# Two tiles' relative-position bands loaded as one overlapping stretch in the second attention layer

## What is computed

```
rel = Q_BLOCK + i - m
bias = rel_bias[relative_bucket(rel * dilation)]      # one number for each head and distance
s = einsum(q, k) * scale + bias
s = where(valid, s, NEG_INF)
lse = logsumexp(s);  p = exp(s - lse);  o = einsum(p, v)
o = sum over groups of softmax(lse over groups) * o
```

## Time and profile before

| what | us |
|---|---|
| median of 3 launches (lowest, highest) | 759.71 (758.87, 760.59) |
| the profiled execution's own time | 757.09 |
| its span | 755.3 |
| PE busy in the span | 744.8 (99%) |
| DVE, ACT, POOL busy | 531.9, 416.7, 175.4 |
| TensorE's mean granted clock | 0.998 of full speed |

### The profile page before, as it was taken

The page is one execution under the profiler, slowest core; times in us unless marked ns, Lnnn a source line. Parts: engine busy times, 40 slices in busy tenths (PEclk is TensorE's granted clock), DMA queues, the critical chain, the costliest instruction groups (busy, mean ns, idle before and its releaser), DMA issues.

```text
span 755.3 us, 13376 instructions
## 1 busy us (share of the span) xinstructions
PE 744.8 (99%) x4616; PEld 639.5 (85%) x4616; DVE 531.9 (70%) x766; ACT 416.7 (55%) x619; POOL 175.4 (23%) x298
## 2 busy tenths in 40 slices
PE   9999999999999999999999999999999999999996
PEld 7999987888888888999898898898878888888884
DVE  5888997776766657777777677677557675666653
ACT  4766667444343344865855867766576434433421
POOL 1000001225100000146664664666502000000000
PEclk9999999999999999999999999999999999999999
DMA  8645585699976675559798897897743797767602
GB/s 251 198 126 162 181 245 186 187 275 231 239 250 202 184 223 136 164 157 242 182 219 175 207 190 194 190 223 210 242 140 98 252 277 217 213 192 233 228 14 56
DMA packets 190756, 147.16 MB, mean 195 GB/s; under 512 B 38521, under 2 KB 179425, under 8 KB 190721
## 3 DMA queue, kind: packets, MB, share of 16 engines
q1 hardware_dynamic: 153344, 131.45, 57.0%
q10 hardware_dynamic: 30592, 7.84, 6.4%
q0 software_dynamic: 6784, 7.41, 6.1%
HBM read 138.02 MB, written 1.11 MB: 184 GB/s over the span
## 4 chain that ended last, share of the span: by engine, by line
PE 61%; issue 16%; POOL 10%; DMA 7%; DVE 3%; ACT 1%; POOLq 1%; SPq 0%; DVEq 0%; ACTq 0%
PE ps L1283 16%; PE ps L1284 15%; PE ps L1285 15%; DMA ones<-bias_rows 4%; POOL work L480 4%; POOL work L499 2%; PE ps L1289 2%; PE ps L1291 2%; PE ps L1290 2%; POOL ones L482 2%; DMA work<-work 2%; POOL work L497 2%; DVE w_lo L852 1%; PE ps L1360 1%; PE ps L1377 1%
## 5 line engine op out<-in xcount | busy, mean ns | idle before, releaser
L852 DVE TENSOR_TENSOR w_lo<-raw,w_hi 128x2048 fp32r<-128x2048 f32 (+2 forms) x144 | 279.8, 1961 | 70.7 <-ACT w_hi L542 70.7
L542 ACT ACTIVATE w_hi<-raw 128x2048 fp32r<-128x2048 f32 (+2 forms) x144 | 233.2, 1639 | 99.4 <-DMA raw<-in_w_kv_b 38.0
L1283 PE MATMUL ps<-w_hi,xt 128*128 128x512 f32 x352 | 137.6, 391 | 0.0
L1285 PE MATMUL ps<-w_hi,xt 128*128 128x512 f32 x352 | 137.0, 389 | 0.0
L1284 PE MATMUL ps<-w_lo,xt 128*128 128x512 f32 x352 | 137.0, 389 | 0.0
L716 ACT ACTIVATE work<-ps,stat 128x256 f32<-128x256 f32 x44 | 21.0, 477 | 155.4 <-PE ps L1285 151.2
L449 POOL TENSOR_SCALAR stat<-stat 128x1 f32<-128x1 f32 x15 | 9.6, 639 | 405.8 <-ACT work L558 381.7
L1283 PE MATMUL ps<-w_hi,ot 128*128 128x512 f32 x240 | 95.0, 396 | 0.1
L1284 PE MATMUL ps<-w_lo,ot 128*128 128x512 f32 x240 | 93.6, 390 | 0.0
L1285 PE MATMUL ps<-w_hi,ot 128*128 128x512 f32 x240 | 93.5, 390 | 0.0
L480 POOL DMA_DIRECT2D work<-bias_rows x128 | 74.9, 587 | 43.5 <-DVE ot L1135 26.7
(11 more groups left out here) (157 smaller groups left out, 1274.2 us busy)
## 6 DMA issues: line engine op xcount, KB each, us to landing
raw<-in_w_gate_up SPq DMA_DIRECT2D x88, 512.0 KB, 5.0
raw<-in_w_kv_b SPq DMA_DIRECT2D x96, 256.0 KB, 4.5
raw<-in_w_down SPq DMA_DIRECT2D x22, 1024.0 KB, 5.2
raw<-in_w_q_b SPq DMA_DIRECT2D x48, 256.0 KB, 4.6
raw<-in_w_qkv_a SPq DMA_DIRECT2D x23, 512.0 KB, 5.2
raw<-in_w_o_a SPq DMA_DIRECT2D x4, 1024.0 KB, 6.9
work<-bias_rows POOLq DMA_DIRECT2D x128, 32.0 KB, 3.6
raw<-in_w_o_b SPq DMA_DIRECT2D x4, 1024.0 KB, 5.2
```

What stands on the lines that cost most here:

```text
L542: act.activation(w_hi[:, s % CUT, 0:size(s)], raw[:, s % RAW, 0:size(s)], ACT.Copy).then_inc(hi_made, 1)
L852: dve.tensor_tensor(w_lo[:, c, 0:n], raw[:, s % RAW, 0:n], w_hi[:, c, 0:n].bitcast(F32), ALU.subtract).then_inc(lo_made, 1)
L1283: mm(out, xs[0], ws[0], start=start, stop=False)
L1285: return mm(out, xs[1], ws[0], start=False, stop=stop)
```

## The change

The two tiles' bands become one stretch of `SPAN` = 64 + 32 = 96 words for each run: `band` is now [128, 4 runs, 96], and tile t reads words 32t to 32t + 63 of each run. The diagonal stretch becomes 96 words in the same way and has room of its own in `work`, for all heads. A head has four transfers of 32 partitions of 4 runs of 96 words (48 KB) and four of 32 partitions of one run of 96 words (12 KB). The additions have the same shapes. The wait for `rows_done` ahead of the loop is gone, since `ones` is no longer overwritten. `work` is 32 words a partition smaller.

```
-WORK = 6912
+WORK = 6880
+SPAN = RUN + HR * (NT - 1)
...
-                         [[(2 * R - 1) * 2 * RUN, NH], [1, HR], [HR, NT], [2 * RUN, R], [1, RUN]]) for r in range(R)]
+                         [[(2 * R - 1) * 2 * RUN, NH], [1, HR], [2 * RUN, R], [1, SPAN]]) for r in range(R)]
...
-        band = carve(NT * SEQ).rearrange("p (t s) -> p t s", t=NT)
-        early_band, own_band = (v.rearrange("p (t n) -> p t n", t=NT) for v in (halves_in[:, 0:NT * RUN], ones[:, :]))
+        band = carve(R * SPAN).rearrange("p (c s) -> p c s", c=R)
+        own_band = carve(SPAN)
...
-                    for t in range(NT):
-                        pool.dma_start(band[at_, t].rearrange("p (c n) -> p c n", c=R),
-                                       bands[r][ds(h, 1)][:, :, t].rearrange("h m c n -> (h m) c n")).then_inc(band_in, 16)
-                    pool.dma_start(own_[at_], own_bands[ds(h, 1)].rearrange("h m t n -> (h m) t n")
-                                   ).then_inc(band_in, 16)
-                pool.wait_ge(band_in, (h * 16 + 16) * (R * (NT + 1)))
+                    pool.dma_start(band[at_], bands[r][ds(h, 1)].rearrange("h m c n -> (h m) c n")).then_inc(band_in, 16)
+                    pool.dma_start(own_band[at_], own_bands[ds(h, 1)].rearrange("h m n -> (h m) n")).then_inc(band_in, 16)
+                pool.wait_ge(band_in, (h * 16 + 16) * (2 * R))
...
-                    distances = band[:, t, ::-1].rearrange("p (c u n) -> p u c n", c=R, u=NT)
+                    reach = slice(HR * t, HR * t + RUN)
+                    distances = band[:, ::-1, reach][:, :, ::-1].rearrange("p c (u n) -> p u c n", u=NT)
...
-            pool.wait_ge(rows_done, 2)
```

More of the change, by code:

```diff
@@ L130, in build @@
         bands = [bass.AP(bias_rows.tensor, bias_rows.offset + 2 * RUN * r,
-                         [[(2 * R - 1) * 2 * RUN, NH], [1, HR], [HR, NT], [2 * RUN, R], [1, RUN]]) for r in range(R)]
+                         [[(2 * R - 1) * 2 * RUN, NH], [1, HR], [2 * RUN, R], [1, SPAN]]) for r in range(R)]
         own_bands = bass.AP(bias_rows.tensor, bias_rows.offset + 2 * RUN * (R - 1),
-                            [[(2 * R - 1) * 2 * RUN, NH], [1, HR], [HR, NT], [1, RUN]])
+                            [[(2 * R - 1) * 2 * RUN, NH], [1, HR], [1, SPAN]])
         raw = sb("raw", [P, RAW, UNIT])
@@ L495, in head_bias @@
                     to, blocked = part(bias[b], t), part(mask_b, t)
-                    distances = band[:, t, ::-1].rearrange("p (c u n) -> p u c n", c=R, u=NT)
+                    reach = slice(HR * t, HR * t + RUN)
+                    distances = band[:, ::-1, reach][:, :, ::-1].rearrange("p c (u n) -> p u c n", u=NT)
                     pool.tensor_tensor(to[0], blocked[0], distances[:, 0:t + 1], ALU.add)
-                    distances = own_[:, t:t + 1, ::-1].rearrange("p o (u n) -> p u o n", u=NT)
+                    distances = own_band[:, reach][:, ::-1].rearrange("p (o u n) -> p u o n", o=1, u=NT)
                     inst = pool.tensor_tensor(to[1], blocked[1], distances[:, 0:t + 1].broadcast_to(
```

1 line of the change is left out of this document (removed).

## The result

| | kernel before | changed kernel |
|---|---|---|
| median of 22 launches each (lowest, highest) | 758.65 (754.59, 761.97) | 760.84 (759.45, 762.96) |
| the profiled execution's own time | 757.09 | 760.09 |
| its span | 755.3 | 758.3 |

The ratio is 1.0034, with a 95% interval of 1.0019 to 1.0048: the change makes the kernel slower by 0.34%, about 2.6 us (the two medians lie 2.2 us apart). The forecast was a gain of 2.4 us. The launches of the kernel before spread over 7.4 us and those of the changed kernel over 3.5; of the kernel before there is one profile, so what its other launches looked like inside is not known. A second set on another chip gave 1.0044 (1.0026 to 1.0062).

The account below looks back on a forecast made before the run. PE was taken to bound the kernel, busy 744.8 of 755.3 us. Gains of 1.59 us (pair 6, last transposes) and 0.8 (pairs 1 to 3) made 2.4: 759.71 - 2.4 = 757.3 us, range 755.9 to 759.7.

Parts of the forecast that it names:

- What bounds the kernel: Layer two's attention: PE is full, 28.70 us is its own length of a pair, POOL can return only what PE loses.
- Four issues less a head: POOL's transfers: 2.3 us less issuing, landing kept at 5.01 us, so a head takes 12.2 us instead of 14.54.
- The lead, and the DVE waits go to nothing: Attention: bias ready 10 to 13 us before DVE's `peaks` wants it; DVE's three waits, 14.6 us in all, vanish.
- What this returns: Attention on PE: 0.99 us of pair 6, 0.60 at the last transposes, and 0.8 of pairs 1 to 3's 1.02.
- the loss isn't there in ordinary launches: Rival: the pause in head 10 was an accident of the profiled execution; about 759.3 us, chance 0.18.
- Nothing behind it takes it back: Behind the attention: PE's list is fixed, DVE and ACT were idle there, so the 1.59 us stays gained.
- The slower rival: The pause stands before POOL's 133rd transfer, now the third `load_post`, with no lead: +4.0 us, 763.7, chance 0.06.
- The additions: POOL's additions read runs 96 words apart instead of 64; even 1 us more on each of four fits the lead.
- the collision: Each pair: POOL's additions behind `peaks` meet DVE's `w_lo`, 0.5 us of DVE; counted as nothing, bound 3.5 us.

Follow-up runs that it names:

- the kernels of 9.99 us: The changed kernel with one of head 1's transfers split, or with 8, 40, 116 or 750 more transfers on POOL: 759.31, 759.69, 758.71, 759.13, 1098.75 us.

## Why the prediction was wrong, step by step

**What bounds the kernel**: right. PE's own length of a pair, 28.70 us, is what all pairs but two now show, and those read 28.75 and 28.78.

**Four issues less a head**: right in direction, short in size. A head took 4.70 + 2.93 us for issues and landing against 4.7 + 5.01 expected. The 5.01 was kept from heads of twelve transfers; in the loop with eight the landings that POOL waited for took 1.7 to 3.8 us. Heads 0 and 1, outside the loop and also with eight, took 5.40 and 4.24, and with five larger transfers a head it was up to 6.1, so what shortens them is not shown.

**The lead, and the DVE waits go to nothing**: right. DVE waits for POOL nowhere, POOL waits 60.8 us for DVE's peaks.

**What this returns**: 1.59 + 0.8 = 2.4 expected, 2.72 measured from pair 0 to the outputs. The size was right, and of the cause only a part. I laid the loss on 0.4 us a pair of a POOL that is too slow, with the pause on top. But with twelve transfers a head and pauses of 1.79 us in head 6 and 5.93 in head 12 the attention takes the same 218.3 us, pairs 1 to 3 included; with 3.49 in head 3 and 6.81 in head 12 it takes 222.3. So it is the place of a pause, and its length, that decide, against a lead that eight transfers make large and twelve leave small. That the pace of twelve transfers a head costs 0.4 us a pair by itself is a second step that didn't hold: a kernel with that pace and its pauses elsewhere doesn't lose it. What exactly lengthened pairs 1 to 3 in the kernel before, I can't say. The rival "the loss isn't there in ordinary launches" had half of this: it said that without the pause POOL would be late nowhere that counts.

**"Nothing behind it takes it back"**: this is the step that failed. It looked at the lists of PE, DVE and ACT behind the attention and not at POOL's third `load_post`, for which DVE and through it PE wait, although has DVE waiting for it. The runs show in its place that this transfer, now POOL's 133rd, went out 3.40 us late, and that moving it alone to ScalarE gives 4.7 us back. The account of the first profile, from the kernel before to the changed one: attention and start of launch -2.83 (554.20 for 557.03 as the end of the last outputs, each its start plus 0.64), the wait of PE +4.34 (7.51 us from outputs to transposes became 11.85), the half clock +2.52 (6.50 to 9.02 from these transposes to the third), which makes +4.03 at the third; then 0.1 less until DVE's last instruction, and an end of 3.4 in place of 4.3 us. That is +3.0, the difference of the spans.

**The slower rival**, "the pause goes by a count of transfers", had the mechanism, the place and the transfer's number. It got 0.06 and should have had far more: with 132 transfers ahead of the pause in the one profile at hand, and 132 in the changed kernel ahead of a transfer without slack, the coincidence was exact, and against it the prediction had only that a single pause could as well go by bytes, runs or time. Its price was mis-sized in two terms that nearly cancel. It took the old pause's 6.86 us where 3.40 came, and PE's wait of 6.4 where 4.3 came; and it left out the clock, 1.5 to 2.5 us. It gave 763.7 (+4.0 us on the kernel before), and 760.84 was measured (+2.6 by the ratio, +3.0 in the two profiles).

**The additions**, `w_lo` and the collision: right at no cost. Pairs 0 and 3 to 6 stayed at 28.70.

**The range** of 755.9 to 759.7 left out the slower cases by intent, with 0.09 for them.

What stays open. Why the count begins behind the second `load_post` in most kernels and behind head 1 in those with 116 or more small transfers; why the pause is 0.4 to 6.9 us long; why a second one came after 72 or 116 transfers with twelve a head; and what POOL does in it. The queues q8 and q14, which carry instructions, moved none during the pause of the kernel before (451 to 459 us), and otherwise had theirs at nearly the same places with and without a pause, which speaks against the fetch of code. That the pause and the closing DRAIN are one upkeep of POOL's queue is the reading that fits: the DRAIN counts the transfers from the last pause on. But the pauses' own lengths don't follow that count, and the kernels of 9.99 us need a further rule.

## What to carry over

Count the transfers of a GpSimd queue in a launch. If the trace has an idle time on POOL that ends in an issue and has no releaser, find the number of that transfer, and work out which transfer will have this number after the edit: it should be one with microseconds of slack. A transfer on which a serial stretch waits (a vector of gains between two blocks) belongs on a queue of ScalarE or SyncE where that engine is idle. But look at the end of the program too: with both loads moved away the time was 760.27 us all the same, since POOL's closing DRAIN took 11.13 us, and one small transfer in POOL's idle time put that right. And a wait of PE of 4.2 us cost another 1.5 to 2.5 us in clock.

## What the hardware showed that I had not expected

- POOL pauses for 0.4 to 6.9 us before a transfer, the first time 128 transfers of 32 partitions behind the second `load_post` in twelve kernels, and 31 transfers of 128 partitions in another.
- The end of a program, from the last computation through stores that landed as before, took 3.4 us or 8.2 to 9.3 us (4.3 in the kernel before), within 0.1 us the same in both profiles of the three kernels that have two; one more transfer of 1 KB in POOL's idle time made it 3.5 instead of 9.3, and the launch 5.6 us shorter by the ratios.
- POOL's closing DRAIN took 0.67 us and 0.082 us for each transfer it had issued from its last pause on, over 1 to 128 transfers in fifteen profiles; in five others it took 9.99 us whatever that number was.
- PE's standstill of 4.2 us was followed by a stretch of 3.4 us (three profiles) or 6.8 us (one) at the 1.2 GHz level, at a cost of 1.5 to 2.5 us. With matmuls in its place the clock stayed at 2.4 GHz.
- Transfers of 48 KB landed in 3.6 us (median), as those of 32 KB had the earlier trace rows, and those of 12 KB in 3.7.
